# A depthwise convolution in eight phases instead of four: all eight channel chunks on TensorE, tap matrices from ScalarE's queue, four stores moved

## The reference, cut to what matters

```python
def conformer_conv_module(h, w_pw1, b_pw1, w_dw, b_dw, ln_g, ln_b, w_pw2, b_pw2):
    a = h @ w_pw1 + b_pw1
    u = a[..., :CONV_CH] * jax.nn.sigmoid(a[..., CONV_CH:])
    y = lax.conv_general_dilated(            # causal, width 31, one filter per channel
        u, w_dw[:, None, :].astype(u.dtype), window_strides=(1,),
        padding=[(CONV_WIDTH - 1, 0)],
        dimension_numbers=('NWC', 'WIO', 'NWC'),
        feature_group_count=CONV_CH) + b_dw
    y = jax.nn.silu(layer_norm(y, ln_g, ln_b))    # mean and variance over the 1024 channels
    return y @ w_pw2 + b_pw2
```

## Time and profile before

| what | value |
|---|---|
| median of the runs | 1828.2 us |
| the profiled execution's own time | 1828.89 us |
| its span, first to last instruction | 1827.1 us |
| mean granted TensorE clock | 0.996 of full |
| TensorE matmul busy | 1808.8 us, 99% |
| VectorE busy | 1020.5 us, 56% |
| ScalarE busy | 644.1 us, 35% |
| memory traffic | 179.08 MB read, 5.24 MB written |

### The profile page before, as it was taken

The page is one execution under the profiler, slowest core; times in us unless marked ns, Lnnn a source line. Parts: engine busy times, 40 slices in busy tenths (PEclk is TensorE's granted clock), DMA queues, the critical chain, the costliest instruction groups (busy, mean ns, idle before and its releaser), DMA issues.

```text
span 1827.1 us, 26277 instructions
## 1 busy us (share of the span) xinstructions
PE 1808.8 (99%) x9934; PEld 1508.4 (83%) x9941; DVE 1020.5 (56%) x1484; ACT 644.1 (35%) x977; POOL 31.2 (2%) x60
## 2 busy tenths in 40 slices
PE   9999999999999999999999999999998999999999
PEld 7888888887698888888888888888887988888887
DVE  6534434589767434434774344347898774344345
ACT  5322313455744223222442232224414542222223
POOL 1000000022000000000000000000000000000000
PEclk9999999999999999999999999999998999999999
DMA  6333333422032333333333333333544333333331
GB/s 205 116 96 102 92 101 92 119 86 79 10 96 93 102 93 92 104 92 102 106 94 102 92 92 104 93 103 104 180 162 138 93 94 102 92 92 104 93 102 58
DMA packets 64078, 186.09 MB, mean 102 GB/s; under 512 B 7264, under 2 KB 19168, under 8 KB 64000
## 3 DMA queue, kind: packets, MB, share of 16 engines
q1 hardware_dynamic: 61824, 182.69, 32.7%
q0 software_dynamic: 1600, 1.52, 0.3%
q10 hardware_dynamic: 576, 0.79, 0.1%
HBM read 179.08 MB, written 5.24 MB: 101 GB/s over the span
## 4 chain that ended last, share of the span: by engine, by line
PE 92%; DVE 5%; issue 1%; ACT 1%; DMA 0%; ACTq 0%; SPq 0%; DVEq 0%
PE bank L401 27%; PE bank L402 27%; PE bank L403 27%; PE bank L494 4%; DVE qT L1608 2%; PE bank L499 2%; DVE w_lo L1259 1%; PE bank L762 1%; PE bank L794 1%; PE bank L738 1%; PE bank L428 1%; PE bank L777 0%; PE bank L420 0%; PE bank L857 0%; PE bank L441 0%
## 5 line engine op out<-in xcount | busy, mean ns | idle before, releaser
L1259 DVE TENSOR_TENSOR w_lo<-w_raw,w_hi 128x1024 fp32r<-128x1024 f32 x302 | 369.2, 1225 | 417.2 <-ACT w_hi L971 406.6
L401 PE MATMUL bank<-x_hi,w_hi 128*128 128x512 f32 x1432 | 558.9, 390 | 0.0
L402 PE MATMUL bank<-x_lo,w_hi 128*128 128x512 f32 x1432 | 557.2, 389 | 0.0
L403 PE MATMUL bank<-x_hi,w_lo 128*128 128x512 f32 x1432 | 557.2, 389 | 0.0
L971 ACT ACTIVATE w_hi<-w_raw 128x1024 fp32r<-128x1024 f32 x302 | 317.1, 1054 | 559.9 <-PE bank L403 547.4
L401 PE MATMUL bank<-a_hi,w_hi 128*128 128x512 f32 (+1 forms) x894 | 331.5, 371 | 1.1 <-issue 1.1
L402 PE MATMUL bank<-a_lo,w_hi 128*128 128x512 f32 (+1 forms) x894 | 329.6, 369 | 0.0
L403 PE MATMUL bank<-a_hi,w_lo 128*128 128x512 f32 (+1 forms) x894 | 329.5, 369 | 0.0
L403 PEld LDWEIGHTS bank<-x_hi,w_lo 128*128 128x128 f32 x1432 | 268.8, 188 | 56.3
L401 PEld LDWEIGHTS bank<-x_hi,w_hi 128*128 128x128 f32 x1432 | 268.8, 188 | 56.2 <-issue 0.7
L402 PEld LDWEIGHTS bank<-x_lo,w_hi 128*128 128x128 f32 x1432 | 268.8, 188 | 55.2
(11 more groups left out here) (206 smaller groups left out, 1322.1 us busy)
## 6 DMA issues: line engine op xcount, KB each, us to landing
w_raw<-stream SPq DMA_DIRECT2D x312, 512.0 KB, 3.6
f_out<-mats_in SPq DMA_DIRECT2D x8, 576.0 KB, 5.6
tap_matrix<-mats_in SPq DMA_DIRECT2D x4, 576.0 KB, 7.3
h_resid<-xT SPq DMA_DIRECT2D x8, 256.0 KB, 6.0
qT<-stream SPq DMA_DIRECT2D x8, 256.0 KB, 6.2
u_scratch<-V SPq DMA_DIRECT2D x6, 256.0 KB, 2.2
a_lo<-u_scratch SPq DMA_DIRECT2D x6, 256.0 KB, 2.7
qT<-z_scratch SPq DMA_DIRECT2D x6, 256.0 KB, 3.6
```

Of the source, the lines that this page charges most:

```text
L401: nc.tensor.matmul(out, lw[0], lx[0], start=first, stop=False)
L402: nc.tensor.matmul(out, lw[0], lx[1], start=False, stop=False)
L403: return nc.tensor.matmul(out, lw[1], lx[0], start=False, stop=last)
L1259: nc.vector.tensor_tensor(w_lo[:, s, :], raw[:, s, :], w_hi[:, s, :].bitcast(F32), ALU.subtract).then_inc(s_lo, 1)
```

## The change: what it does

The phases go from 4 to 8, and all eight chunks are convolved on TensorE (`NAT` and `taps` are gone, `CONVS = 8`). A group is now 16 channels x 8 phases = 128 rows of 64 steps; there are 8 groups or 4 pairs to a chunk and 5 shifts. A chunk is 4 x 5 x 4 = 80 matmuls on 64 columns of data, where it was 72 on 128. A tap matrix for a pair of groups is 320 KB, 32 of them where there were 12 of 576 KB; 14 buffers hold them where there were 5. Eight are loaded from SP's queue at the start of the feed-forward block ahead of the module, six at the old place, and the other 18 by DMA issues that stand in ScalarE's program behind its slot conversions. `u` and `zg` travel in runs of 256 bytes. The early mean is over three chunks; their subtraction moves into the second-last pair of slots. SP stores the first four centred chunks ahead of the last chunk's `u`. The sums of groups write one half of the array's columns and not two in turn.

The diff, cut to its core:

```diff
-PH = 4
+PH = 8
-NAT = 2
-CONVS = KD - NAT
-EARLY = 4
+CONVS = KD
+EARLY = 3
...
-        conv_out = [two_banks[i] for i in (3, 2, 3, 2, 3, 0)]
+        conv_out = [two_banks[i] for i in (3, 3, 3, 3, 3, 0, 1, 3)]
...
             conv_turn = (PW1 + 2 * RING) // RING
-            loads(2, conv_turn)
+            loads(2, FFN2 // RING + 1)
+            first_matrices(FREE_MATS)
+            loads(FFN2 // RING + 1, conv_turn)
             for j in range(KD):
                 n = PW1 + 2 * RING + 2 * j
                 load(n, n % RING)
-                if j >= RING:
-                    load_matrices(j - RING + 1)
-                load(n + 1, (n + 1) % RING)
+                if j < KD - 1:
+                    load(n + 1, (n + 1) % RING)
                 if j == 0:
                     sp.wait_ge(s_root, 3 * 4 + 1)
-                    load_matrices(0)
-                if j >= NAT:
-                    store_u(j - NAT)
-                    load_groups(j - NAT)
-            load_matrices(CONVS - 1)
-            for i in range(EARLY):
-                store_z(i)
-            sp.wait_ge(s_nat, NAT)
-            for i in range(EARLY):
+                    first_matrices(F_MATS)
+                if j == KD - 1:
+                    for i in range(EARLY + 1):
+                        store_z(i)
+                store_u(j)
+                load_groups(j)
+            load(n + 1, (n + 1) % RING)
+            sp.wait_ge(s_cv, PAIRS * 6)
+            for i in range(EARLY + 1):
                 load_y(i)
...
                 def sum_groups(out, src, first, last):
 
                     for g in range(GROUPS):
-                        for part in range(2):
-                            to = slice(part * HALF, (part + 1) * HALF)
-                            ins = nc.tensor.matmul(out[to, 0:PH], src[:, g, to], same_q[:, 0:PH],
-                                                   start=(first and g == 0), stop=(last and g == GROUPS - 1),
-                                                   skip_group_check=True)
+                        ins = nc.tensor.matmul(out[0:NT, 0:PH], src[:, g, :], same_q[:, 0:PH],
+                                               start=(first and g == 0), stop=(last and g == GROUPS - 1),
+                                               skip_group_check=True)
...
                 first_body(n0, sub)
-                body(n0 + 6, 2)
                 for i in range(EARLY):
-                    for n in range(2 * i + 7, 2 * i + 9):
+                    for n in range(2 * i + 6, 2 * i + 8):
                         body(n0 + n, n % RING)
                     convolve(i)
-                body(n0 + 15, 3)
+                body(n0 + 12, 0)
                 sum_early()
-                convolve(4, range(0, 1))
+                body(n0 + 13, 1)
+                convolve(EARLY)
+                for n in range(14, 16):
+                    body(n0 + n, n % RING)
+                for i in range(EARLY + 1, CONVS - 1):
+                    convolve(i)
                 pe.wait_ge(s_m0, 1)
-                spread_phases(BCAST, m0).then_inc(s_m0bc, 1)
-                convolve(4, range(1, 2))
-                convolve(5, range(0, 1))
-                pe.wait_ge(s_nat, NAT)
-                sum_direct(BCAST, nat_sum, 1, True).then_inc(s_dlmm, 1)
-                sum_rest(4)
-                convolve(5, range(1, 2))
-                sum_squares(True)
-                sum_rest(5)
-                sum_squares(False)
+                pe.wait_ge(s_rest, 2)
+                sum_groups(BCAST, rest, True, False)
+                convolve(CONVS - 1)
+                sum_centred(6)
+                pe.wait_ge(s_root, 3 * sub + 1)
+                pe.wait_ge(s_zsqadd, CONVS - 2)
+                sum_groups(STAT, zsq_sum, True, False)
+                sum_centred(7).then_inc(s_dlmm, 1)
+                pe.wait_ge(s_zsq, CONVS)
+                sum_groups(STAT, zsq[(CONVS - 1) % 2], False, True).then_inc(s_sqmm, 1)
...
                 for q in range(PH):
-                    ins = nc.tensor.matmul(out[:, q * NT:(q + 1) * NT], v[:, q:q + 1].broadcast_to([P, P]),
-                                           ident[:, :], start=True, stop=True)
+                    ins = nc.tensor.matmul(out[:, q * NT:(q + 1) * NT], v[:, q:q + 1].broadcast_to([NT, P]),
+                                           ident[0:NT, 0:NT], start=True, stop=True)
...
+                def load_matrices(i, count=PAIRS):
+                    for k in range(MATS + PAIRS * i, MATS + PAIRS * i + count):
+                        act.wait_ge(s_cv, k - MATS + 1)
+                        act.dma_start(mats[k % MATS], mats_in[k // PAIRS, k % PAIRS, :, :]
+                                      ).then_inc(s_mats[k % MATS], 16)
+
                 for j in range(KD):
                     for e in range(2):
                         n = n0 + 2 * j + e
-                        if n >= n0 + RING - 1:
+                        if n0 + RING - 1 <= n < n0 + PW1_SLOTS - 1:
                             next_slot(n, n % RING, n // RING)
+                        if e == 0 and j >= RING:
+                            load_matrices(j - RING)
```

More of the change, by code:

```diff
@@ L171, in build_program @@
-        u_nat = [yv[:, NAT * T + c * (CW - 1 + T):NAT * T + (c + 1) * (CW - 1 + T)] for c in range(NAT)]
-        nat_acc = [y[:, KD - NAT + c, :] for c in range(NAT)]
-        nat_sq, nat_sum = nat_acc, sq[:, 1, :]
+        early = sq[:, 0, :].rearrange("p (j n) -> p j n", n=NT)
+        rest = sq[:, 1, :].rearrange("p (g n) -> p g n", g=GROUPS)
+        mats = [room[:, i * MAT:(i + 1) * MAT]
+                for room, first, count in ((spare, 0, 1), (more, 0, 2), (fv, 0, 1), (yv, 0, Y_MATS), (fv, 1, 5))
+                for i in range(first, first + count)]
@@ L174, in build_program @@
+        MATS = len(mats)
+        F_MATS = 3, 9, 10, 11, 12, 13
+        FREE_MATS = [i for i in range(MATS) if i not in F_MATS]
         first_raw = qT[:, :, :].rearrange("p a n -> p (a n)").rearrange("p (s n) -> p s n", s=RING)
@@ L234, in build_program @@
         s_ud = [sem(f"u_in_dram{i}") for i in range(2)]
-        s_ug = [sem(f"u_groups_loaded{i}") for i in range(2)]
+        s_ug = [sem(f"u_groups_loaded{i}") for i in range(CONVS)]
         s_zd = [sem(f"z_in_dram{i}") for i in range(4)]
@@ L879, in sum_early @@
                     last.then_inc(s_m0mm, 1)
-                def sum_rest(j):
-                    pe.wait_ge(s_zc, j + 1)
-                    sum_groups(BCAST, zg[j], False, j == CONVS - 1).then_inc(s_dlmm, 1)
-                def sum_direct(out, src, ready, first):
-                    pe.wait_ge(s_nsum, ready)
-                    for q in range(PH):
-                        for part in range(2):
-                            to = slice(part * HALF, (part + 1) * HALF)
-                            ins = nc.tensor.matmul(out[to, q:q + 1], src[:, q * NT + to.start:q * NT + to.stop],
-                                                   ones[:, 0:1], start=(first and q == 0), stop=False,
-                                                   skip_group_check=True)
-                    return ins
@@ L918, in convolution @@
-                convolve(5, range(0, 1))
-                pe.wait_ge(s_nat, NAT)
-                sum_direct(BCAST, nat_sum, 1, True).then_inc(s_dlmm, 1)
-                sum_rest(4)
-                convolve(5, range(1, 2))
-                sum_squares(True)
-                sum_rest(5)
-                sum_squares(False)
-            def spread_phases(out, v):
-                for q in range(PH):
-                    ins = nc.tensor.matmul(out[:, q * NT:(q + 1) * NT], ident[:, q:q + 1].broadcast_to([P, P]),
-                                           v[:, :], start=True, stop=True)
-                return ins
+                body(n0 + 13, 1)
@@ L1658, in conv @@
-                bias_less_mean(4)
-                dve.wait_ge(s_nsq, NAT)
-                nc.vector.tensor_tensor(nat_sq[0], nat_sq[0], nat_sq[1], ALU.add).then_inc(s_nsum, 1)
+                        if (j, e) == (KD - 2, 0):
+                            dve.wait_ge(s_m0mm, 1)
+                            nc.vector.tensor_scalar(m0[:, :], BCAST[:, 0:NT], 1.0 / (EARLY * P), None, ALU.mult
+                                                    ).then_inc(s_m0, 1)
+                            dve.wait_ge(s_m0, 1)
+                            for i in range(EARLY):
+                                centre(i)
+                            bias_less_mean(3)
+                            bias_less_mean(4)
@@ L1661, in conv @@
+                        if (j, e) == (KD - 1, 0):
+                            centred(3)
+                            add_squares(1)
+                            add_squares(2)
+                            bias_less_mean(6)
+                    gate(j)
+                    if EARLY <= j < 2 * EARLY:
+                        biased(j - EARLY)
+                        add_early(j - EARLY)
+                next_slot(n, n % RING)
                 centred(4)
```

(3 more changed lines are left out.)

211 lines of the change are left out of this document (85 added, 126 removed).

## The result

The changed kernel takes 1831.9 us (median of 18 runs, 1829.43 to 1838.01) against 1827.86 us of the kernel before in the same series: a ratio of 1.0024, 95% interval 1.0017 to 1.0031. I had forecast 1816.5 us and a range of 1809 to 1830 us. The forecast gain didn't come; the time is 0.24% longer, by little but clear of noise. The profiled execution took 1830.32 us, with a span of 1828.5 us. It lies 1.6 us under its median and that of the kernel before (1828.89 us) 1.0 us above its own, so the two traces show 1.4 of the 4.0 us between the medians.

A forecast was written before the change was run, and what follows sets the result against it. TensorE was taken to bound the kernel up to the last slot, a chain of waits behind it. The next product 11.8 us earlier turned 1828.9 into 1817.1 us, 1816.4 against the median: forecast 1816.5 us, range 1809 to 1830.

The forecast's parts named there:

- Up to the last slot: Stretch until the last slot ends: four chunks save 6.1 us, the early mean adds 0.7 us, end at 1370.7 us.
- a round no shorter: Rival, convolution on TensorE: a round of four matmuls stays at 0.109 us; 1832 us, no change; chance 0.11.
- row halves in turn: Rival, convolution's weight loads: the two row halves load one behind the other, 0.120 us a round; 1835 us, slower; chance 0.07.
- Behind the last slot: From the last slot's end to the next product: 22.5 us, so that product starts at 1393.2 us, 11.8 us earlier.
- Chunks 4 to 6 ... 0.44 + 120 x 0.060 = 7.6 us: TensorE right behind the last slot: three chunks in a row take 120 rounds of 0.060 us plus 0.44 us, 7.6 us.
- chunk 7 in 2.8 us: Last chunk's convolution on TensorE, once its `u` is loaded: 40 rounds of 0.060 us plus 0.44 us, 2.84 us.
- The four stored chunks ahead of the last `u` cost issue time while VectorE is still busy with the gate: SP's queue ahead of the last `u`: these stores only cost issue time during the gate; listed under what costs nothing.
- the rival of short runs: Store and load of `u`: 256-byte transfers take twice the time, four stores ahead delay as much again; 1819 to 1822 us; chance 0.08.
- E: The time at which the last of the sixteen slots ends, forecast at 1370.7 us instead of 1376.1 us.
- E + 9.0 us: Forecast time at which the last `u` is loaded and chunk 7 can start, 0.4 us of it added for 256-byte runs.
- I keep the 0.75 us: Sums and spreadings ahead of the next product: the lower clock costs 0.75 us, as the second spreading's excess did before.
- My rival of the low clock: Behind the last slot the clock stays low, doubling all TensorE work there; 1833 us, 4.9 us later; chance 0.06.

The follow-up runs named there:

- experiment one: Changed kernel with the four stores of centred chunks put back behind the last chunk's store and load of `u`: 1834.35 us, 1.0035 to the kernel before.
- experiment ten: Reordered kernel with wide products and one matmul per spreading, plus fourth z store, y loads and slot load put off until chunk 7's first quarter: 1821.47 us, 0.9966.
- the two last: Reordered kernels with one matmul per spreading, one with wide and one with small products, traffic put off until chunk 7's first quarter: 1821.47 and 1823.36 us.
- the best version: The same run as experiment ten: wide products, one matmul per spreading, traffic put off until chunk 7's first quarter is done; 1821.47 us, 0.9966.

## Why the prediction was wrong

**Up to the last slot: right.** A round of four quadrant matmuls takes 0.058 us (ten rounds of chunk 4 from 1371.67 to 1372.25 us; 0.060 assumed), a chunk 2.72 us, the last slot ends 0.3 us off. The rivals of a round no shorter and of row halves in turn are out. So is the floor of some 25 ns between starts that the Trainium skill, "TensorE: Matmul & The Clock Gate", section "Wait — 56ns, not 53.3ns?", gives, for matmuls in different quadrants: here 160 records in 2.51 us are under 16 ns apart.

**Behind the last slot: wrong by 13.3 us**, in three steps.

*"Chunks 4 to 6 ... 0.44 + 120 x 0.060 = 7.6 us"* and *chunk 7 in 2.8 us* failed. The price of a chunk that I had read between slots doesn't hold for chunks in a row, since it takes no account of where instructions come from. A chunk has 80 matmuls of four instructions, 1.25 blocks, and the stops end 3.3 us apart at best; at the new pace a block is used up in under 2 us. Chunks 4 to 6 and the sum took 13.2 us up to the wait for `u` instead of 8.6, and chunk 7 took 5.9 us instead of 2.8 (2.82 us of it standing still). Before, no such stop stands behind the last slot: 72 matmuls, 288 instructions, took 3.9 us, which is 3.5 us for a block, by this reckoning just slow enough. The Trainium skill, "Runtime: NRT & Kernel Launch", section "Instruction fetch mechanics", has the 16 KB block and says that crossing to the next is mostly hidden; the packets agree with the size, and the idle times of 0.5 to 2.8 us disagree with the rest.

*"The four stored chunks ahead of the last `u` cost issue time while VectorE is still busy with the gate"* failed: the gate was done at 1373.8 us, SP came to the store at 1375.0 us, and store and load took 9.6 instead of 5.8 us behind 1 MB of stores. This was the second half of the rival of short runs. (Its sum was wrong: with store and load both twice as long chunk 7 starts at E + 14.4 us; E + 11.9 counts one of the two.) Its first half, the runs of 256 bytes themselves, is out: with chunk 4 early and the stores behind, store and load took 3.27 and 2.85 us, and chunk 7 began at my E + 9.0 us. The stores alone would have cost some 4.3 us (13.6 against the 9.3 us of experiment one), but TensorE was no earlier (0.40 us of waiting was left), so the two delays hid each other, and undoing one gained nothing.

*"I keep the 0.75 us"* for the clock failed: the clock was low for 17 us in one piece, where before it was low in pieces of 3.4 us. Four sums took 6.9 us instead of 3.85, two spreadings 7.0 us instead of 3.55, what follows 2.4 us instead of 3.3: 5.6 us together. The prices at full clock were right: a sum of 16 records takes 1.08 us there, 0.95 us to the next start (experiment ten; 0.96 forecast), and a spreading's 3.5 us are twice the 1.78 forecast. My rival of the low clock had its place here, but spoke against itself by "the new order has no such gap"; the stops for instructions are such gaps. That they lower the clock is not shown. In every run but the two last the first low stretch behind the last slot begins no more than 2.4 us from the end of a stop of TensorE, but stops stand every few us there. In those two it begins at 1388.8 and 1390.0 us, in the sums and spreadings, 10.6 and 8.1 us behind the last stop, so it falls without a stop just ahead as well. What lowers it stays open.

The sum of the misses: 0.3 (last slot) + 4.6 (from there to chunk 7) + 3.1 (inside it) + 5.6 (behind it) = 13.6 us: 1406.8 instead of 1393.2 us. With the late `u` and the stop inside chunk 7 gone, one stop of 0.87 us left ahead of it, and a part of the clock's share gone, the best version starts the next product at 1395.7 us.

## What to carry to other kernels

Where a change makes matmuls shorter without making them fewer, work out the bytes of instructions per us as one does for data: straight code that runs back to back needs its next block in time, and a price read where long products stand between the short ones doesn't hold. An idle time "issue" in the middle of equal instructions, with a packet of the instruction queue landing just ahead of its end, is the sign; spread such code among long products, and keep bulk transfers away from it. When two delays end at nearly the same time, undoing one shows nothing: try both together before a theory is dropped.

## What the runs showed of the hardware that I had not expected

From the start of one block of TensorE's instructions, where a stop marks it, to the landing of the next it took 2.0 to 2.7 us while other transfers took no more than 0.52 of the DMA engines' time, and 2.1 to 5.9 us while they took 0.7 or more; from the landing it was 1.0 to 1.7 us more to the first matmul. Four float32 records in four quadrants, 64 columns each way, take 0.058 us together. One DMA issue on SP's queue, 0.33 us for a slot's load just before, took 3.86 us behind two stores of 256 KB in runs of 256 bytes, and 3.3 to 4.1 us in three other runs that have the same three stores in a row.
